# First attention outputs gated in halves, and the compressed branch's operations spread, in a two-block transformer kernel

## The reference

```
gates = sigmoid(proj[..., N_QH * HEAD_DIM:])            # three-branch attention
p_c = masked_softmax(q . k_cmp);  o_c = p_c . v_cmp     # at most 15 compressed blocks
o = g0 * o_c + g1 * o_selected + g2 * o_window;         return o @ w_out

o = softmax(q . k * scale + forget sums, causal) . v    # forget-gate attention
o = softmax(q_lat . kv_lat, selected keys) . v          # latent attention
x = layer_norm(alpha * x + (silu(gate) * o) @ w_out)    # both
```

## Time and profile before

| | us |
|---|---|
| runs, median of 3 (lowest, highest) | 1340.21 (1339.82, 1340.5) |
| the profiled execution, its own time | 1334.75 |
| its span, first to last instruction | 1333.0 |
| PE busy (share of the span) | 1280.7 (96%) |
| DVE busy | 873.1 (65%) |
| ACT busy | 613.0 (46%) |
| mean granted clock of PE, of full speed | 0.987 |

### The profile page before, as it was taken

The page is one execution under the profiler, slowest core; times in us unless marked ns, Lnnn a source line. Parts: engine busy times, 40 slices in busy tenths (PEclk is TensorE's granted clock), DMA queues, the critical chain, the costliest instruction groups (busy, mean ns, idle before and its releaser), DMA issues.

```text
span 1333.0 us, 16476 instructions
## 1 busy us (share of the span) xinstructions
PE 1280.7 (96%) x6717; PEld 1085.8 (81%) x6717; DVE 873.1 (65%) x1302; ACT 613.0 (46%) x838; POOL 24.1 (2%) x37
## 2 busy tenths in 40 slices
PE   6999999989999999999999988999999999999987
PEld 5888888978888888878888875778888899988876
DVE  6655557786655557685856668675555575667885
ACT  6444436525444445543544456554444443535361
POOL 2000000200000000000000000000000000000000
PEclk9999999999999999999999999999999999999899
DMA  9655545434655655456565340166555685346201
GB/s 305 223 189 184 186 152 181 160 127 143 205 189 189 189 190 172 155 179 222 188 198 181 102 158 1 46 207 190 189 190 169 118 234 165 130 163 217 96 1 63
DMA packets 158810, 218.16 MB, mean 164 GB/s; under 512 B 8256, under 2 KB 110992, under 8 KB 158736
## 3 DMA queue, kind: packets, MB, share of 16 engines
q1 hardware_dynamic: 156880, 212.56, 50.2%
q0 software_dynamic: 1376, 3.71, 0.9%
q10 hardware_dynamic: 480, 0.85, 0.2%
HBM read 216.04 MB, written 1.05 MB: 163 GB/s over the span
## 4 chain that ended last, share of the span: by engine, by line
PE 87%; DVE 7%; ACT 3%; issue 2%; DMA 1%; SPq 0%; DVEq 0%
PE PS L679 24%; PE PS L682 24%; PE PS L680 24%; PE PS L714 2%; PE PS L715 2%; PE PS L800 1%; ACT whi L1490 1%; PE PS L721 1%; DVE wlo L2010 1%; PE PS L992 1%; PE PS L699 1%; DMA raw<-in_ffn_w_in_dram 1%; PE PS L1275 1%; PE PS L1261 1%; PE PS L1288 1%
## 5 line engine op out<-in xcount | busy, mean ns | idle before, releaser
L2010 DVE TENSOR_TENSOR wlo<-raw,whi 128x2048 fp32r<-128x2048 f32 (+4 forms) x206 | 457.5, 2231 | 122.7 <-ACT whi L1490 121.9
L1490 ACT ACTIVATE whi<-raw 128x2048 fp32r<-128x2048 f32 (+4 forms) x206 | 381.4, 1864 | 64.4 <-DMA raw<-in_fox_w_in_dram 33.8
L679 PE MATMUL PS<-whi,XL 128*128 128x512 f32 (+3 forms) x992 | 385.4, 389 | 9.1 <-DVE XL L2057 3.5
L680 PE MATMUL PS<-wlo,XH 128*128 128x512 f32 (+3 forms) x992 | 379.3, 383 | 0.0
L682 PE MATMUL PS<-whi,XH 128*128 128x512 f32 (+3 forms) x992 | 264.6, 384 | 0.0
L679 PEld LDWEIGHTS PS<-whi,XL 128*128 128x128 f32 x992 | 187.1, 189 | 44.3 <-issue 3.9
L680 PEld LDWEIGHTS PS<-wlo,XH 128*128 128x128 f32 x992 | 187.2, 189 | 32.7
L682 PEld LDWEIGHTS PS<-whi,XH 128*128 128x128 f32 x992 | 185.1, 189 | 35.0
L1544 ACT ACTIVATE scr<-PS,rn 128x256 f32<-128x256 f32 x88 | 41.7, 474 | 227.0 <-PE PS L682 223.9
L679 PE MATMUL PS<-whi,GL 128*128 128x512 f32 x320 | 125.6, 392 | 0.0
L680 PE MATMUL PS<-wlo,GH 128*128 128x512 f32 x320 | 124.7, 390 | 0.0
(11 more groups left out here) (375 smaller groups left out, 1349.6 us busy)
## 6 DMA issues: line engine op xcount, KB each, us to landing
raw<-in_ffn_w_in_dram SPq DMA_DIRECT2D x174, 512.0 KB, 5.0
raw<-in_ffn_w_out_dram SPq DMA_DIRECT2D x88, 512.0 KB, 5.0
raw<-in_fox_w_in_dram SPq DMA_DIRECT2D x24, 512.0 KB, 8.2
raw<-in_a_w_in_dram SPq DMA_DIRECT2D x16, 512.0 KB, 4.6
raw<-in_dsa_w_in_dram SPq DMA_DIRECT2D x16, 512.0 KB, 5.9
raw<-in_kv_w_dram SPq DMA_DIRECT2D x12, 512.0 KB, 4.3
raw<-in_fox_w_in_dram SPq DMA_DIRECT2D x12, 344.0 KB, 5.2
raw<-in_a_w_out_dram SPq DMA_DIRECT2D x8, 512.0 KB, 4.5
```

Source lines behind the costliest of these rows:

```text
L679: mm(o, xl, wh, start=start and i == 0, stop=False, skip_group_check=True)
L680: mm(o, xh, wl, start=False, stop=False, skip_group_check=True)
L1490: A(whi[:, p % SLOTS, 0:n], raw[:, p % SLOTS, 0:n], ACT.Copy).then_inc(hi_done, 1)
L2010: V.tensor_tensor(wlo[:, p % SLOTS, 0:n], raw[:, p % SLOTS, 0:n], whi[:, p % SLOTS, 0:n].bitcast(F32), ALU.subtract).then_inc(lo_done, 1)
```

## The change

Seven things, all in the order or the size of operations; nothing of the arithmetic is new. (1) In `attend_four`, PE's `value(2)` waits only for the first half of the gated output (`z_half`), and `value(3)` for the second. (2) On DVE, in both stages, `raw_z` and `silu_gate` come in halves: first output half, first gate half (as soon as ACT's first sigmoid is there, `sig_half`), second gate half, copy of unit 2, second output half, copy of unit 3. (3) In the forget-gate stage DVE's weight piece ahead of the gate product goes behind the first output's low part; so does one in the latent stage. (4) In the latent stage ACT splits pieces `first + 13` and `first + 14` before unit 0's copies and the last piece behind the first output's high part. (5) In the three-branch stage `cmp_least` and `cmp_shares` are taken apart (`cmp_masked`, `cmp_least`, `cmp_shifted`, `cmp_weights`, `cmp_shares`) and spread over the units; `cmp_exp(0)` moves ahead of unit 1's exponentials, `cmp_exp(1)` from unit 1 to unit 3. (6) PE waits there for `cs_raw`, the masked scores, where it waited for the shifted ones. (7) The first tile's output is split in halves, and the first values of the second tile wait for the first half (`n_free`).

```diff
@@ PE, attend_four
                 turn_p(3)
+                pe.wait_ge(z_half, zstage[stage])
+                value(2)
                 pe.wait_ge(z_raw, 2 * (zstage[stage] - 1) + 1)
-                value(2)
                 value(3)
@@ PE, three-branch stage
-                pe.wait_ge(cs_exp, t + 3)
+                pe.wait_ge(cs_exp, 2 * t + 2)
...
                 if k == KVH:
+                    pe.wait_ge(n_free, 1)
+                elif k == KVH + 4:
                     pe.wait_ge(z_ready, 1)
...
                 if k == 0:
-                    pe.wait_ge(cs_neg, 1)
+                    pe.wait_ge(cs_raw, 1)
                 n_turn(k)
                 if k == 3:
-                    pe.wait_ge(cs_exp, 3)
+                    pe.wait_ge(cs_exp, 2)
...
                 elif k == 2:
-                    pe.wait_ge(cs_neg, 3)
+                    pe.wait_ge(cs_raw, 2)
                     cmp_turned(0, 7)
@@ ACT
-                split_to(min(chunk_end(stage, c) + AHEAD, first_piece["dsa_out"] + (4 if c == 5 else 1))
+                split_to(min(chunk_end(stage, c) + AHEAD, first_piece["dsa_out"] + (3 if c == 5 else 1))
...
-                A(XH[:, :, t * P:t * P + P], O_ps, ACT.Copy).then_inc(z_hi, 1)
+                if t == 0:
+                    A(XH[:, 0:4, 0:P], O_ps[:, 0:4, :], ACT.Copy).then_inc(n_half, 1)
+                    A(XH[:, 4:8, 0:P], O_ps[:, 4:8, :], ACT.Copy).then_inc(z_hi, 1)
+                else:
+                    A(XH[:, :, t * P:t * P + P], O_ps, ACT.Copy).then_inc(z_hi, 1)
...
             n_exps(0)
+            cmp_exp(0)
             act.wait_ge(q_ps, 3)
             q_gained(1, 6)
             n_exps(1)
-            cmp_exp(0)
...
-                if k == 1:
+                if k == 3:
                     cmp_exp(1)
...
-                A(f_gate[:, m:m + 2, :], two(o), ACT.Sigmoid)
+                A(f_gate[:, m:m + 2, :], two(o), ACT.Sigmoid).then_inc(sig_half, 1)
...
             exps_four("dsa", 1)
+            split_to(first + 15)
             first_of_pt("dsa", 0)
...
             dsa_parts(0, 0)
+            split_to(NP)
             dsa_parts(1, 0)
@@ DVE, three-branch stage
+            cmp_masked(0, 4)
+            cmp_least(0)
             n_least_of(0)
+            cmp_shifted(0)
             n_least_of(1)
             q_gained(1, 7)
-            cmp_least(0, 4)
             for k in range(len(n_units)):
                 n_scale(k)
+                if k == 5:
+                    cmp_weights(1)
                 if k + 2 < len(n_units):
                     n_least_of(k + 2)
                 if k == KVH + 1:
-                    low_of_z("nsa", 0, O_ps)
+                    dve.wait_ge(n_half, 1)
+                    V.tensor_tensor(XL[:, 0:4, 0:P], O_ps[:, 0:4, :], XH[:, 0:4, 0:P].bitcast(F32), ALU.subtract)\
+                        .then_inc(n_free, 1)
                 n_second_of_pt(k)
                 if k == 0:
+                    cmp_weights(0)
+                elif k == 1:
                     cmp_shares(0)
-                elif k == 1:
-                    cmp_least(1, 7)
+                    cmp_masked(1, 7)
+                elif k == 2:
+                    cmp_least(1)
                 elif k == 3:
+                    cmp_shifted(1)
+                elif k == KVH + 1:
+                    dve.wait_ge(z_hi, 1)
+                    V.tensor_tensor(XL[:, 4:8, 0:P], O_ps[:, 4:8, :], XH[:, 4:8, 0:P].bitcast(F32), ALU.subtract)\
+                        .then_inc(z_ready, 1)
+                elif k == 6:
                     cmp_shares(1)
@@ DVE, both attention stages
+            def silu_first(stage, c, m, n):
+
+                dve.wait_ge(sig_half, n)
+                g = f_gate[:, m:m + 2, :]
+                V.tensor_tensor(g, g, two(bank_of(stage, c, 0)), ALU.mult)
+
+            def silu_second(stage, c, m):
+
+                dve.wait_ge(chunk_act, first_chunk[stage] + c + 1)
+                g = f_gate[:, m + 2:m + 4, :]
+                V.tensor_tensor(g, g, two(bank_of(stage, c, 1)), ALU.mult).then_inc(chunk_dve, 1)
...
+            def raw_first(stage):
+
+                dve.wait_ge(pv_done, unit0[stage] + 1)
+                V.tensor_tensor(z_mix[:, 0:4, :], O_ps[:, 0:4, :], f_gate[:, 0:4, 0:P], ALU.mult).then_inc(z_half, 1)
+
+            def raw_second(stage):
+
+                dve.wait_ge(pv_done, unit0[stage] + 2)
+                dve.wait_ge(chunk_dve, first_chunk[stage] + len(stages[stage][1]))
+                V.tensor_tensor(z_mix[:, 4:8, :], O_ps[:, 4:8, :], f_gate[:, 4:8, 0:P], ALU.mult).then_inc(z_raw, 1)
...
             scale_four("fox", 3)
-            silu_gate("fox", 8, 4)
-            dve.wait_ge(pv_done, unit0["fox"] + 2)
-            raw_z("fox", 0)
+            raw_first("fox")
+            silu_first("fox", 8, 4, 2)
+            silu_second("fox", 8, 4)
             second_of_pt("fox", 2)
+            raw_second("fox")
             second_of_pt("fox", 3)
...
             scale_four("dsa", 3)
-            split_to(first + 14)
-            silu_gate("dsa", 5, 4)
-            dve.wait_ge(pv_done, unit0["dsa"] + 2)
-            raw_z("dsa", 0)
+            raw_first("dsa")
+            silu_first("dsa", 5, 4, 4)
+            silu_second("dsa", 5, 4)
             second_of_pt("dsa", 2)
+            raw_second("dsa")
             second_of_pt("dsa", 3)
```

More of the change, by code:

```diff
@@ L351, in program @@
         z_raw = sem("z_raw")
+        z_half = sem("z_half")
+        sig_half = sem("sig_half")
         z_hi = sem("z_hi")
@@ L354, in program @@
         cs_ps = sem("cs_ps")
+        cs_raw = sem("cs_raw")
         cs_neg = sem("cs_neg")
+        n_half = sem("n_half")
+        n_free = sem("n_free")
         cs_exp = sem("cs_exp")
@@ L2542, in q_gained, with cmp_masked, cmp_least, cmp_shifted @@
                                 qgain[:, 0:1], None, ALU.mult).then_inc(qT_dve, 1)
-            def cmp_least(t, bank):
+            def cmp_masked(t, bank):
                 dve.wait_ge(cs_ps, t + 1)
+                V.tensor_tensor(n_cs[:, t, :, :], PS[:, bank, :].rearrange("p (h n) -> p h n", h=QH),
+                                cmask[:, t:t + 1, :].to_broadcast([P, QH, 32]), ALU.add).then_inc(cs_raw, 1)
+            def cmp_least(t):
+                dve.wait_ge(cs_raw, t + 1)
+                link(V.tensor_reduce(cm_min, n_cs[:, t, :, :], AX, ALU.min))
+            def cmp_shifted(t):
                 s = n_cs[:, t, :, :]
-                link(V.tensor_tensor(s, PS[:, bank, :].rearrange("p (h n) -> p h n", h=QH),
-                                     cmask[:, t:t + 1, :].to_broadcast([P, QH, 32]), ALU.add))
-                link(V.tensor_reduce(cm_min, s, AX, ALU.min))
                 V.tensor_tensor(s, s, cm_min.unsqueeze(2).to_broadcast([P, QH, 32]), ALU.subtract).then_inc(cs_neg, 1)
[L2553 to L2557, removed]
+            def cmp_weights(t):
+                dve.wait_ge(cs_exp, (1, 3)[t])
+                link(V.tensor_reduce(cm_sum, n_cs[:, t, :, :], AX, ALU.add))
                 link(V.reciprocal(cm_sum, cm_sum))
@@ L2561, in cmp_shares @@
                                             op0=ALU.mult, op1=ALU.mult))
+            def cmp_shares(t):
+                s = n_cs[:, t, :, :]
                 V.tensor_tensor(s, s, cm_sum.unsqueeze(2).to_broadcast([P, QH, 32]), ALU.mult).then_inc(cs_neg, 1)
```

## The result

The changed kernel takes **1320.73 us**, the median of 4 runs (1318.74 to 1321.16); the kernel before, run beside it, 1340.01 (1335.25 to 1340.5). The ratio is 0.9879 with a 95% interval of [0.9852, 0.9905]. The forecast was 1327.1 us, with a range from 1325.0 to 1331.5: right in direction, and 6.4 us too little.

A forecast was written before the change was run, and what follows sets the result against it. With TensorE busy 1280.7 of 1333.0 us, only its waits and slow stretches could be won: 3.7 + 1.9 + 5.3 + 2.2 = 13.1 us, from profiled 1334.75 to 1321.6. As a median, 1327.1 us, range 1325.0 to 1331.5.

The forecast's parts named there:

- three-branch stage: Term for the three-branch stage: moved operations and a halved first output let TensorE leave it 3.7 us earlier.
- forget-gate stage: Term for the forget-gate stage: halves and a moved weight piece start the attention values 1.9 us earlier.
- latent stage, wait: Term for the latent-attention stage: TensorE's wait of 5.56 us before the values shrinks by 5.3 us.
- latent stage, clock: Term for the latent-attention stage: the values run at full instead of half clock, winning 2.2 us.
- The starts 792.2, 801.8, 810.0 and 824.1: Three-branch stage: predicted TensorE starts, in us, of the transposes of units 0, 2, 4 and 7.
- The estimate of 12.7 us: Alternative sum, not kept: 0.16 us fixed cost for each of five added VectorE instructions gives 12.7 instead of 13.1 us.
- the last step: Whole kernel: from profiled time to median, the same 5.5 us difference assumed after the change, giving 1327.1 us.
- A: Rival: the granted clock still falls, here or at another place that has run fast; 1329.3 us, chance 0.10.
- B: Rival: three-branch stage gains only 2.0 us, a moved small operation becoming the wait between units 3 and 7; 1328.8, chance 0.12.
- C: Rival: splits moved back in the last stage come late, putting 2.2 us on the path; 1329.3 at most, chance 0.10.
- D: Rival: the change works but the time is lost later in a transfer-bound stretch; about 1340 us, chance 0.03.
- E: Rival, slower: in the last stage a weight piece lands late and ScalarE's early splits hold up copies; 1343, chance 0.02.

The follow-up runs named there:

- nsa_order2: Kernel before with only the three-branch stage's moved operations, first output left whole, run a second time: 1331.69 us, ratio 0.9961.
- dsa_halves: Kernel before with only the latent-attention stage's output and gate in halves on VectorE, ScalarE's splits as before: 1333.85 us, ratio 0.9982.
- fill_before: Kernel before plus 16 unread matmuls in TensorE's waits ahead of units 0, 1, 2 and 4 of the three-branch stage: 1333.2 us, ratio 0.9968.
- both_att_fill: Kernel before with both attention stages changed and 16 unread matmuls in the three-branch stage's waits: 1322.91 us, ratio 0.9895.
- both_att: Kernel before with the change in both attention stages only, the three-branch stage as before: 1326.55 us, ratio 0.9924.
- dsa_splits: Kernel before with only ScalarE's weight splits of the latent-attention stage moved, no halves: 1331.51 us, ratio 0.9957.

## Why the prediction was right, and where it was wrong

Read along the two profiled executions, term by term:

| | worked out | measured | from |
|---|---|---|---|
| three-branch stage | 3.7 | 3.46 | 844.75 to 841.29 |
| forget-gate stage | 1.9 | 1.86 | wait 2.21 to 0.35 |
| latent stage, wait | 5.3 | 5.2 | wait 5.56 to 0.36 |
| latent stage, clock | 2.2 | 2.27 | 6.08 to 3.81 |
| the rest of the program | 0 | 1.4 | low clock near 1240 to 1247 only before (2.8), near 1092 to 1096 only after (-1.5) |
| sum | 13.1 | 14.15 | 1334.75 to 1320.6 |

The last term is no part of the worked sum: the change touches no instruction at either place, and other profiles have both of the two low stretches (nsa_order2) or neither (dsa_halves).

**Right.** The starts 792.2, 801.8, 810.0 and 824.1 were measured as 792.61, 801.95, 810.15 and 824.28, and the four small terms stand. The moved splits stayed hidden; so did the norm, by 0.72 us where 0.8 were worked out. The halves cost what the rows said: 0.68 or 0.69 us each at 0.60 from start to start. The estimate of 12.7 us charged each added VectorE instruction a fixed 0.16 us, as read off the Trainium skill ("VectorE: DVE Perf Modes", section "The TRN2 errata"). That figure is part of one instruction's own length, and there the trace agrees with the page: 0.68 or 0.69 us for 512 columns, where the page has 691 ns. But neighbours overlap by 0.08 us here, and the two terms that rest on halves, 1.86 and 5.2 against 1.9 and 5.3, leave at most 0.1 us each for it.

**Wrong: the last step**, "The median of the runs is 1340.21, 5.5 us above the profiled execution; I take the same difference off it". It treated the 5.5 us as a constant of measuring that the changed kernel would have too; measured there, it is 0.1 us (1320.73 against 1320.6). It was for the most part slow TensorE that the profiled execution happened not to have. In its place: six of eight profiles of the old order run part of the three-branch stage at the lower granted clock, which costs up to 6.9 us (844.75 to 851.67) and 4.3 on average. The change ends that, and filler alone, with the old order, wins 4.3 (fill_before) or about 4 (both_att_fill over both_att). So the three-branch term was mis-sized against the median: 3.7 worked out, 8.1 by the mean ends of the stage, 7.1 to 7.9 by the ratios of the kernels with that stage alone. With 10.2 for the two attention stages (both_att) that makes 17 to 18 us; the changed kernel's ratios, 0.9879 and 0.9864, give 16 and 18. The 19.3 between the medians is that and four runs of before that lay high in its range (1340.01 against the usual 1337.05).

The clock was looked up for one stretch, the one that was slow in the profile; the waits of 1.4 to 1.9 us in the earlier trace rows were priced as time alone. The evidence against a constant stood there: the spread of the three runs was 0.7 us and the profiled one lay 5.5 below their median.

**The rivals.** A (the clock falls all the same) did not come: 1.00 in the window of the values. B (a moved small operation becomes the new wait between units 3 and 7) did not: unit 7 starts 3.5 us early. Its ground, that VectorE has no idle time there, was misread: in the trace of before VectorE is idle three times between 808 and 825, 0.65, 2.07 and 0.64 us, for want of scores. C (a late split) did not: no product of `dsa_out` waits for a low part. D (the time is lost later) and E (a piece lands late) are excluded by the profile after: the whole span is 14.1 us shorter, and ACT's two splits ran at 1268.65 without a wait. More gain than worked out was given no chance at all.

## What to carry to other kernels

Before taking a profile as the typical execution, compare its own time with the median of the runs: a gap well above their spread means that some stretch ran differently, and a second profile of the same kernel shows which. Price a wait of TensorE between short matmuls twice, by its length and by the clock behind it, in the stages where the profile has it as well as where it happened not to. Unread matmuls in such a wait tell with one more kernel whether the clock is at stake (here it took 11 executions, since the gain was 0.3%), and where the order can't be changed they are a remedy.

## What the runs showed that was not expected

The two courses of the same program can be told apart before the three-branch stage's first scores are there. Over windows of 4 us, before:

```profile
764.00:768.00 4.00, 4.00 (x12) 3.23 (x12) 2.64 (x10) 3.46 (x3) 0.00 (x0) 0.50 0.00 0
786.00:790.00 4.00, 2.97 (x28) 2.14 (x26) 3.23 (x4) 2.52 (x15) 0.00 (x0) 0.98 0.53 172
796.00:800.00 4.00, 3.12 (x32) 2.39 (x31) 3.83 (x8) 2.12 (x13) 0.00 (x0) 1.00 0.00 0
```

and the unchanged copy:

```profile
764.00:768.00 4.00, 4.00 (x28) 3.67 (x28) 2.82 (x11) 2.70 (x4) 0.00 (x0) 1.00 0.01 4
786.00:790.00 4.00, 3.88 (x28) 2.76 (x26) 2.32 (x2) 2.52 (x15) 0.00 (x0) 0.72 0.49 169
796.00:800.00 4.00, 4.00 (x19) 3.58 (x17) 3.75 (x8) 3.39 (x17) 0.00 (x0) 0.50 0.00 0
```

The clock is at one of two levels, 0.50 or 1.00 (1.2 or 2.4 GHz); 0.72, 0.76 and 0.81 are averages over stretches at either. Both kernels have a low stretch from about 782 us on. It ends near 786 before and near 788 in the copy, and this small difference grows: the scores at 786.11 take 1.22 us in the copy and 0.75 before, VectorE starts the mask (L2548) at 790.71 and not at 789.79, and TensorE's wait ahead of unit 0 is 2.29 us and not 1.38. In all six low profiles that wait is 2.18 to 2.64 us and the clock falls right behind it, between 794 and 796; in the two others it is 1.38 and 1.36 and the clock stays. In the changed kernel, with the low stretch as long as in the copy, it is 0.28. That the first scores start at 790.43 in both hides the difference, since they wait for ScalarE. The parting goes further back: the low stretch at 764 to 768 is in before and dsa_splits and in none of the six. What makes it, no run here shows.

One wait alone does not decide: in the forget-gate stage before, one of 2.21 us passed at 1.00, which was the forecast's ground for calling such waits safe, and the waits of 1.81 us ahead of unit 4 passed at 1.00 before and stand ahead of a fall at about 819 in the copy.

That the clock of one kernel differs from run to run is also what the Trainium skill says ("TensorE: Matmul & The Clock Gate", section "What's actually happening"); it puts the price of the slow start at under 1% of a typical kernel's span. The trace agrees in size: 6.9 us between two executions, 0.5%, in one stage. It also calls the slow level the default, which activity releases. The trace agrees in so far as the clock stays at 1.00 where fill_before keeps TensorE busy with 16 matmuls that nobody reads, and falls in the copy, which comes in at the same level and has none.
